# Modulation columns reordered on VectorE, both high-half weight rings at 128 bytes modulo 512, latents normed in place

## The reference, cut to what matters

```
block 1: h = rms_norm(x);  proj = h @ w_in
         q, kv = rms_norm(q_a) @ wq_b, rms_norm(kv_a) @ wkv_b     (the "latents" q_a, kv_a: 512 wide)
         y_mla = attention(...);  y_rwkv = bidirectional RWKV-7 scan(...)
         merged = sig(gate_mla) * (y_mla*silu(z)) @ w_br_mla + sig(gate_rwkv) * (y_rwkv*silu(z)) @ w_br_rwkv
         x = x + rms_norm(merged @ w_out)
block 2: z = x @ w_in_2;  conv (31 taps, 1024 channels), multiscale pool, Fourier mix -> mixed
         x = layer_norm(a*x + mixed @ w_out_2)
         x = layer_norm(a*x + (silu(x@w_gate)*(x@w_up)) @ w_down + sig(x@w_ple_gate)*(p@w_ple))
block 3: mod = silu(c) @ w_ada + b_ada                      (c: 1 x 2048, w_ada: 2048 x 12288)
         h = rmsnorm(x)*(1+sc1)+sh1;  two attentions;  x = x + g1*(merged @ w_out_3)
         h2 = rmsnorm(x)*(1+sc2)+sh2;  x = x + g2*conv_ffn(h2);  rmsnorm(x)
```

## Time and profile before

| | us |
|---|---|
| median of 3 runs | 3669.42 (3668.66 to 3690.33) |
| the profiled execution | 3681.26 |
| its span | 3679.9 |
| PE busy | 3510.1 (95%) |
| DVE busy | 2293.6 (62%) |
| ACT busy | 1451.3 (39%) |

### The profile page before, as it was taken

The page is one execution under the profiler, slowest core; times in us unless marked ns, Lnnn a source line. Parts: engine busy times, 40 slices in busy tenths (PEclk is TensorE's granted clock), DMA queues, the critical chain, the costliest instruction groups (busy, mean ns, idle before and its releaser), DMA issues.

```text
span 3679.9 us, 64349 instructions
## 1 busy us (share of the span) xinstructions
PE 3510.1 (95%) x26444; PEld 3332.6 (91%) x26444; DVE 2293.6 (62%) x3097; ACT 1451.3 (39%) x1732; POOL 76.6 (2%) x156
## 2 busy tenths in 40 slices
PE   8999999999997999979999999998998999999998
PEld 8997888888887985979999999998987899999998
DVE  7775655545547869766765554545566667777645
ACT  5441223223222400644444433345355454444443
POOL 0000100000000000000000000000000000000000
PEclk9999999999998999989999999999999999999999
DMA  8757611111135864547765555543442455555554
GB/s 305 261 186 304 227 49 48 48 60 66 68 126 217 342 248 148 185 160 274 274 228 184 187 191 194 195 172 127 162 150 101 154 189 185 193 185 191 195 193 151
DMA packets 91876, 655.24 MB, mean 178 GB/s; under 512 B 10193, under 2 KB 10833, under 8 KB 13138
## 3 DMA queue, kind: packets, MB, share of 16 engines
q1 hardware_dynamic: 74736, 540.05, 40.8%
q0 software_dynamic: 14400, 104.86, 7.4%
q10 hardware_dynamic: 2594, 8.15, 0.6%
HBM read 650.93 MB, written 2.10 MB: 177 GB/s over the span
## 4 chain that ended last, share of the span: by engine, by line
PE 87%; DVE 7%; ACT 3%; issue 2%; DMA 1%; DVEq 0%; ACTq 0%; SPq 0%
PE ps L465 20%; PE ps L466 19%; PE ps L467 19%; PE ps L628 6%; PE ps L426 5%; PE ps L702 2%; PE ps L496 2%; PE ps L690 2%; PE ps L436 1%; DVE ring_parts L1620 1%; PE ps L511 1%; DMA work<-in_ada 1%; DVE work L1635 1%; PE ps L746 1%; PE ps L737 1%
## 5 line engine op out<-in xcount | busy, mean ns | idle before, releaser
L1620 DVE TENSOR_TENSOR ring_parts<-ring,ring_hi 128x1024 fp32r<-128x1024 f32 x858 | 1032.3, 1224 | 741.6 <-ACT ring_hi L1079 731.0
L1079 ACT ACTIVATE ring_hi<-ring 128x1024 fp32r<-128x1024 f32 x858 | 901.6, 1059 | 1188.5 <-PE ps L467 1139.3
L466 PE MATMUL ps<-h_lo,ring_hi 128*128 128x256 f32 x2624 | 732.9, 279 | 0.0
L465 PE MATMUL ps<-h_hi,ring_hi 128*128 128x256 f32 x2112 | 595.4, 282 | 16.2 <-DVE ring_parts L1620 11.8
L467 PE MATMUL ps<-h_hi,ring_parts 128*128 128x256 f32 x2112 | 589.0, 279 | 0.0
L466 PEld LDWEIGHTS ps<-h_lo,ring_hi 128*128 128x128 f32 x2624 | 497.7, 190 | 1.3 <-issue 1.2
L465 PE MATMUL ps<-x_hi,ring_hi 128*128 128x256 f32 x1664 | 468.3, 281 | 15.7 <-DVE ring_parts L1620 11.2
L466 PE MATMUL ps<-x_lo,ring_hi 128*128 128x256 f32 x1664 | 465.4, 280 | 0.0
L467 PE MATMUL ps<-x_hi,ring_parts 128*128 128x256 f32 x1664 | 465.0, 279 | 0.0
L465 PEld LDWEIGHTS ps<-h_hi,ring_hi 128*128 128x128 f32 x2112 | 398.9, 189 | 19.1 <-DVE ring_parts L1620 13.0
L467 PEld LDWEIGHTS ps<-h_hi,ring_parts 128*128 128x128 f32 x2112 | 398.7, 189 | 0.0
(11 more groups left out here) (442 smaller groups left out, 5731.6 us busy)
## 6 DMA issues: line engine op xcount, KB each, us to landing
ring<-in_weights SPq DMA_DIRECT2D x511, 1024.0 KB, 4.8
work<-in_ada POOLq DMA_DIRECT2D x96, 1024.0 KB, 6.7
work<-in_c_row POOLq DMA_DIRECT2D x4, 1024.0 KB, 5.0
resid<-in_lora ACTq DMA_DIRECT2D x9, 256.0 KB, 3.6
resid<-in_x SPq DMA_DIRECT2D x4, 512.0 KB, 6.2
resid<-in_x ACTq DMA_DIRECT2D x1, 2048.0 KB, 14.6
out<-work SPq DMA_DIRECT2D x4, 512.0 KB, 2.8
con<-in_const ACTq DMA_DIRECT2D x1, 1536.0 KB
```

Of the source, the lines that this page charges most:

```text
L465: mm(o, w_hi[:, k, cols], hi(kc), start=(kc == 0 and m % 2 == 0), stop=False, skip_group_check=True)
L466: mm(o, w_hi[:, k, cols], lo(kc), start=False, stop=False, skip_group_check=True)
L1079: A(high_ring(n)[:, 2 * (e % 2) + half, :], ring[:, n % RING, half * (SLOT // 2):(half + 1) * (SLOT // 2)], ACT.Copy)\
L1620: tt(lo, x, high_ring(n)[:, e % 4, :].bitcast(F32), ALU.subtract).then_inc(S("lo_ready"), 1)
```

## The change

1. QAN and KVAN become the tiles QA and KVA themselves.
2. HI_1 moves from element 18432 to 18336, HI from 35504 to 35488: both at 128 bytes modulo 512, as `ring` is.
3. Run 2: column 40 alone before `first_branch(2)`, 41 alone before `first_branch(3)`; one column in each of the four br_rwkv groups (before: in two); 13 in w_out (before: 12); 13 before the convolution (before: 10).
4. Run 3: the two slots are at 19456 (where the sigmoid of c was) and 8192. Its first load waits for the new semaphore `row_ready` only, which DVE raises after `silu_row(3)`; that step moves forward, from behind `angles(2)` to between the splits of slots 11 and 12 of w_out2. The second load waits for the 16 scaled chunks.
5. ffn2 loop: a column after the first and the third split of each group of four, none ahead of the first split and none at the end of the trip.

```diff
-    QAN, KVAN = w(16384, 4, T), w(17408, 4, T)
+    QAN, KVAN = QA, KVA
-    HI_1, H1_HI = own("ring_hi1", 18432, 4, SLOT // 2), own("h1_hi", 22528, DC, T)
+    HI_1, H1_HI = own("ring_hi1", 18336, 4, SLOT // 2), own("h1_hi", 22528, DC, T)
-    HI = own("ring_hi", 35504, 4, SLOT // 2)
+    HI = own("ring_hi", 35488, 4, SLOT // 2)
-           (in_slots(22528, 2), w(28672, SLOT), w(31296, SLOT)), (in_slots(6144, 2), w(17408, SLOT), w(19456, SLOT))]
+           (in_slots(22528, 2), w(28672, SLOT), w(31296, SLOT)), ([w(19456, SLOT), w(8192, SLOT)], w(17408, SLOT), w(19456, SLOT))]
...
-        def fetch_modulations(run):
+        def fetch_modulations(run, second_free=None):
...
+                if second_free is not None and n == ADA_FIRST[run] + 1:
+                    gp.wait_ge(second_free, DC)
                 gp.dma_start(slots[slot], a["ada"][n]).then_inc(S(f"ada_loaded{slot}"), 16)
...
-        gp.wait_ge(S("scaled"), DC)
-        fetch_modulations(3)
+        gp.wait_ge(S("row_ready"), 1)
+        fetch_modulations(3, S("scaled"))
...
-        modulation(40, 3)
+        modulation(40, 1)
         first_branch(2)
-        modulation(43, 5)
+        modulation(41, 1)
         first_branch(3)
...
-            if j in (1, 2):
-                modulation(47 + j, 1)
+            modulation(42 + j, 1)
         for n in range(14):
             split(so + 2 + n, 1)
-            if n < 12:
-                modulation(50 + n, 1)
+            if n < 13:
+                modulation(46 + n, 1)
...
-        modulation(62, 10)
+        modulation(59, 13)
...
-                split(slot0("w_out2") + 11, 3)
+                split(slot0("w_out2") + 11, 1)
+                silu_row(3)
+                t.give(v.nop(), S("row_ready"))
+                split(slot0("w_out2") + 12, 2)
...
-                silu_row(3)
                 v.wait_ge(S("p_hi"), 1)
...
-                if with_columns:
-                    columns(i, 0, 1)
-                split(slot0("ffn2", 2 * at) + 2, 4, i, 8)
-                v.wait_ge(S("ffn_sig"), i + (at + 1))
-                tt(flat(GU2), bank2(0), flat(GU), ALU.mult).then_inc(read_out[0], 1)
-                if with_columns:
-                    columns(i, 1, 1)
-                split(slot0("ffn2", 2 * at + 1) + 2, 2, i, 8)
-                if with_columns:
-                    columns(i, 2, 1)
-                split(slot0("ffn2", 2 * at + 1) + 4, 2, i, 8)
+                for j in range(2):
+                    for n in range(4):
+                        split(slot0("ffn2", 2 * at + j) + 2 + n, 1, i, 8)
+                        if with_columns and n in (0, 2):
+                            columns(i, 2 * j + n // 2, 1)
+                    if j == 0:
+                        v.wait_ge(S("ffn_sig"), i + (at + 1))
+                        tt(flat(GU2), bank2(0), flat(GU), ALU.mult).then_inc(read_out[0], 1)
...
                 if with_columns:
-                    columns(i, 3, 1)
                     v.wait_ge(S("ada_used"), i * FFN2_COLUMNS + (ADA_FIRST[3] + FFN2_COLUMNS))
```

## The result

| | before | after |
|---|---|---|
| median of 20 runs each | 3677.88 us (3663.55 to 3699.81) | 3699.72 us (3695.20 to 3706.80) |
| ratio, 95% interval | | 1.0052 (1.0040 to 1.0065) |
| the profiled execution | 3681.26 us | 3700.82 us |

The change makes the kernel about 0.5% slower, where 3634 us was forecast; the time lies beyond the range of 3586 to 3670. The edits of the order gained 22 us of the 25 forecast, and the rings did the opposite of what was forecast: 49 us lost, not 17 gained (experiments 1 and 2).

The account below looks back on a forecast made before the run. PE work bounds the kernel (87% of the wait chain), so only PE waits and matmul spacing count. Order terms -24.6 and rings -17.2 give 3639.5 from 3681.3, or 3627.6 from the median; middle 3634 us, range 3586 to 3670.

Parts of the forecast that it names:

- (a): Around br_mla: one column before each branch product shortens PE's waits, -25.6 us; a 13th w_out column costs about +0.3.
- (b): Three more columns before the convolution delay the sum PE needs before pooling: +14.8 us, bounds 4.7 to 19.5.
- (c): Late w_out2: the 2.29 us product of silu_row(3) moves from ahead of the sum PE waits for: -2.3 us.
- (d): First ffn2 trip: without load and column ahead of the splits, PE waits less: -6.3 us, bounds -3.6 and -6.3.
- (e): Later ffn2 trips: columns spread between the splits remove five PE waits: -5.5 us.
- (f): High rings at 128 bytes: matmul spacing of 115.4 ns in the first block and the long stretch, -17.2 us.
- the possible late load: In w_out, with windows moving 336 GB/s at a DMA share of 0.87, a column's load may be late: up to +2 us.
- the slack of 1.9: Before the pooling matmuls: DVE's sum is ready 1.9 us before PE takes it up, absorbing that much delay.
- The upper bound of +36: For the moved high rings: every affected matmul at 118.1 ns would cost +36 us.
- Rival 3: New ring placement behaves like the first block's, over the ffn2 to down3 stages too: +36 us, total 3681; chance 0.13.
- The rival from the Trainium skill: Ring moves do nothing, as TensorE has two independent SBUF read ports: 3645 us (3657 from the profile's side); chance 0.22.
- The two values for before: Whole kernel: 3639.5 us if the long spacing is a state an execution falls into, otherwise 3627.6; middle 3634 taken.

Follow-up runs that it names:

- experiment 1: The changed kernel with the tiles and high rings of the kernel before, so order edits alone; 3648.96 us, ratio 0.9938.
- order_192: The changed kernel with both high rings at 192 bytes modulo 512, latents still in place; 3647.63 us, ratio 0.9943.
- rings_only: The kernel before with both high rings at 128 bytes modulo 512 and latents in place, no order edits; 3720.53 us, ratio 1.0128.
- low_320: order_192 with the low ring at 320 and the high ring at 64 in br_rwkv and w_out; 3646.75 us, one run.
- best_320: order_192 with three of thirteen pre-convolution columns moved elsewhere, the other ten started earlier, low ring at 320, both high rings at 64; 3620.09 us, ratio 0.9844.
- low_192: order_192 with the low ring at 192 and the high ring at 128 in br_rwkv and w_out; 3675.12 us, one run.
- low_256: order_192 with the low ring at 256, the high ring at 64 in the first block and 256 in br_rwkv and w_out; 3686.62 us, one run.
- fine: order_192 with the high ring at 160 in the first block and at 480 elsewhere; 3688.25 us, one run.

## Why the prediction was wrong

By stage, from the first PE instruction of one stage to that of the next (within half a us), in us of the profiled executions. Order_only is the change without the rings, so the column "order" holds the price of the steps (a) to (e), and the last one that of (f). "Order" also holds differences of spacing that no edit of the order made, under equal addresses: the 6.1 of down2 and 7.6 of the ffn2 loop, see below, and the 2.7 of the first row lies ahead of every edit. The rows leave out the 15.4 us behind the last stage, equal in all three:

```
                          before   order_only   order    after   rings
up to the end of br_mla   1130.0    1127.3       -2.7   1130.3    +3.0
br_mla to w_out             70.9      45.2      -25.7     46.4    +1.2
w_out                       95.7      98.7       +3.0     98.3    -0.4
convolution to w_out2      190.7     211.4      +20.7    211.1    -0.3
w_out2                      92.1      92.1        0       92.1     0
w_out2 to ffn2              27.3      25.8       -1.5     24.7    -1.1
ffn2 loop                  537.4     517.2      -20.2    530.7   +13.5
down2                      324.9     318.8       -6.1    327.4    +8.6
block 3 up to down3        957.1     956.7       -0.4    978.4   +21.7
down3                      238.4     238.4        0      244.8    +6.4
```

- **(a), right.** -25.7 measured, -25.6 worked out. In w_out, **+3.0 and not +0.3**: the possible late load came about. In order_only a column waits 2.46 us for its load where the DMA share is 0.97, and PE waits 2.8 us for the last slot (experiment 1). The +2 in the bounds was the better value. The share was 0.87 in the window of the earlier trace rows that the sum looked at; that the denser columns filled it up is argued, not shown.
- **(b), right in kind, too small.** +20.7 against +14.8 and the upper bound of 19.5. The sum took the pace of ten columns, 4.8 us each, for thirteen; the other eleven came at (63.3-4.4)/11 = 5.4 us, and a load took 7.6 us by the median, not 6.4. The rest of the sum holds. From the start of conv_in (1296.2 before, 1270.7 in order_only) DVE's sum is ready after 169.7 and 190.2 us, 20.5 later, and PE takes it up after 171.4 and 190.3, 18.9 later: the slack of 1.9 was there, within 0.3. Half clock after the pause adds 1.8, foreseen as 2.2. The pace is no constant of the order: in order_192, the same order, DVE waits 27.7 us and not 33.5.
- **(c), right.** -1.5 against -2.3; no product of 2.29 us stands ahead of the last sum.
- **(d), (e), right.** The loop became 20.2 us shorter in order_only, but 7.6 of them are a matter of spacing. From 1660 to 1850 us before's busy PE spends 117.1 ns a matmul and order_only's 115.4 (185.67 us/1585 and 190/1646), from 1870 to 2130 117.6 and 115.5 (260/2210 and 260/2252; plain quotients of windows of equal length): 1.5% of 186 us and 1.9% of 260 are 7.6. The rest, 12.6, stands beside -6.3 - 5.5 = -11.8. In (d) the wait is shorter than the 2 to 3 us foreseen, 1.28 in after.
- **(a) to (e) together** make -25.7 + 3.0 + 20.7 - 1.5 - 12.6 = -16.1 us by the stages, where -24.6 was forecast; w_out and (b) are the difference. Between medians it is -22.5, with an interval of -32 to -14 that holds both. That it lies so near the forecast is partly luck.
- **(f), wrong, and nearly the whole error.** The step that failed is: "Since the one placement that never gave the short spacing is 0, I take 115.4 for the first block, ..., and, less surely, 115.4 for the long stretch". It gave -17.2. Measured are +49.1 between medians (rings_only against before) and +52.6 between profiled executions (after against order_only); 17,700 later matmuls lengthened by 118.7-115.6 = 3.1 ns are 55. No row had the relation, and the step gave it the short spacing because it was not the one bad place known; measured is 118.7 ns in every window, the long spacing that the text named as its sign of being wrong. Its term for the first block, -5.7, came to nothing: 118.9 ns at 0 and at 128. The upper bound of +36 was too low too, through the count at the edge of a window: in the earlier trace rows the first block's 118.1, from 45 us, is 118.9, the 117.7 of the long stretch 117.8 and the 115.4 of the others 115.6. With these the bound is 5012 x 1.1 + 12700 x 3.3 = 47, near the 49 measured. **Rival 3** was the right mechanism, with 0.13; it gave 3681, from a bound of 36 where 49 was measured, and from a median of 3669.4, of 3 runs, where 20 runs have 3677.9. What the prediction held for it was weak: the low ring is at 128 in the fast windows of the earlier trace rows as well, so that relation alone decides nothing.
- **The rival from the Trainium skill** (TensorE: Matmul & The Clock Gate, Step-by-step: what each phase is for), (f) at nothing, falls: between after and order_192 only the address of the high weights differs, at equal order and equal clock and a DMA share within 0.02, and 118.7 against 115.6 ns is measured from 1870 to 2400 us. Whether it is the ports of which the page speaks that make the difference, no run shows.
- **The two values for before** (3639.5 or 3627.6) came from a spacing that differs from run to run. Before's 20 runs spread over 36 us, after's over 12 and the five of rings_only over 3. The 1870 to 2400 window has 115.6 ns in order_only and 117.8 in before, at the same places (192, 128). So with the high ring at 192 a stretch has one of two spacings, and at 128 each window seen has the same. That this explains the spread of the times fits, but rests on one profile of each kernel: argued, not shown.

Without the rings the forecast would have been 3669.4 - 24.6 = 3645, and order_only is at 3649, beside a before of 3671.4.

## What to carry to other kernels

The spacing of equal matmuls at full clock is a cost like any wait: count them in a window that is busy throughout, do it for every stage, and treat the place of each operand as one parameter of a pair or triple, to be measured in all its stages before it is believed; a place that no row shows gets the whole range of the spacings seen, not the best one. Compare windows of equal length, or take the matmuls in flight at the edge off the count. Where a refilled ring of two slots feeds an engine, the price of one more step in a stretch is near the time of its load under the traffic of that stretch; starting the engine's part earlier bought nothing with thirteen such steps here. When a kernel's runs spread more than the effect sought, look for a stage that has two spacings in the profiles before taking one profile as the base of a sum.

## What the runs showed of the hardware

- A 128x256 fp32r matmul of the split triples, with the clock at 1.00, starts every 113.3, 115.6, 116.6, 117.8, 118.2, 118.7, 118.9, 119.1 or 120.1 ns in the windows from 1180 us on, depending on where the high ring, the low ring and the features stand. The same values come back under different places, nearly to the count: 4679 matmuls in low_320 and in best_320, 4589 in order_only, 4502 in low_192, low_256 and fine (and 4503 in before), from 1870 to 2400 us.
- One placement can have two of them in one execution: 113.3 and 118.9 ns in low_320, 115.6 and 117.8 in before. The change can come in the middle of a stage. In before's ffn2 loop the spacing is 115.6, 117.8, 115.6 and 117.8 in turn, and each change follows one of the five waits of the earlier trace rows, those that end at 1673, 1766 and 1858 us; the other two, at 1720 and 1812, change nothing (before, PE windows between the waits):

```profile
1640.00:1670.00 30.00, 30.00 (x262) 1.00 0.72 265
1680.00:1710.00 30.00, 30.00 (x257) 1.00 0.67 251
1775.00:1805.00 30.00, 30.00 (x262) 1.00 0.73 269
1870.00:1900.00 30.00, 30.00 (x257) 1.00 0.61 214
```

  In best_320 it goes from 113.3 to 117.8 near 3019 us, where PE does not wait:

```profile
2980.00:3010.00 30.00, 30.00 (x267) 1.00 0.51 178
3025.00:3055.00 30.00, 30.00 (x257) 1.00 0.51 178
```

  So a restart of PE may choose the spacing, but a wait is not needed for a change; what chooses is open, and no run here forces it.
- The pairs seen from 1870 to 2400 us (high, low; features at 0): 192, 128: 115.6 and 117.8. 128, 128: 118.7. 320, 128: 118.2. 480, 128: 117.8. 192, 192: 117.8. 192, 256: 117.8. 192, 320: 113.3. 64, 320: 113.3. From 1180 to 1240 us: 256, 128: 119.1. 128, 192: 116.6. 256, 256: 120.1. 64, 320: 113.3 in low_320 and 117.8 in best_320. No rule is settled by them, and what in the memory makes it is open.
- One load of a modulation slot of 1 MB took 6.4 us by the median in before's ten columns, 7.6 in after's thirteen, 6.5 in order_192's thirteen and 8.4 with the parameters' loads beside it.
- After a pause of 16.4 us PE ran at a granted clock of 0.54 for 3.2 us; after a wait of 1.28 us, in a stretch that was busy otherwise, it ran at 1.00.
